# A gate table in SBUF laid out by token instead of by expert column, in a two-layer transformer kernel on one core

## Chip, cores and metric

The kernel runs on one core of a Trainium2 chip. The metric is the device time of one execution in microseconds; lower is better. Times are medians over several executions.

## The reference, cut to what matters

256 tokens of width 1024 go through two transformer blocks. The first ends with a mixture over 16,384 tiny experts (128 x 128), of which each token takes 16 for each of 8 heads:

```
experts = e1 * 128 + e2                      # 16 per token and head
g   = softmax(best)                          # their gate weights
act = gelu(x . u[experts])                   # one number for each
out = sum over experts of (g * act) * v[experts]
```

The kernel does not gather. It computes gelu(x . u) for all 128 x 128 experts, multiplies by a dense table G of gates that is zero where an expert was not chosen, and multiplies the whole by v. The second block (attention over the sequence, a gated linear attention, cross attention, a gated feed-forward) is not touched by the change.

## The kernel before

Everything is float32, and each matmul is made from three passes of rounded parts. Weights come in 404 blocks of 128 x 1024 float32 (a block is 512 KB) through a ring of four buffers. For each block ScalarE makes the rounded part (`w_hi`, L588) as soon as TensorE has freed the buffer, and the remainder (`w_lo`) is a subtraction on GpSimd (L487) for the blocks of even number in the stages below, and on VectorE (L1043) for the odd ones. In the first of the three stages below, all remainders are GpSimd's.

Experts are ordered so that partition p and column e of the table are one expert. `big` is one buffer of 128 partitions x 32,768 floats that holds G as 128 columns x 256 tokens. Three stages matter.

*The gate stage.* It builds G. For each token VectorE writes two 128 x 128 one-hot matrices (L1365, L1366); TensorE multiplies them (L2003) into a bank of PSUM, four tokens side by side, 128 columns each; ScalarE copies the bank of 512 numbers into G (L868). There are 64 such groups of four tokens. Beside it runs one block of x . u for every two groups, 32 in all (L1643), evacuated with gelu (L843) and stored to DRAM. The order on each engine is written out by hand.

*The V stage.* It takes the 64 columns whose activations are ready. Per column c: VectorE multiplies the activations of 256 tokens with column c of G (L1384), rounds the product into `h_op` (L1391) and writes the remainder (L1393); TensorE multiplies block v[c] with it in 24 matmuls (L2020). `h_op` has two buffers, so the rounding of column c waits until TensorE has finished column c - 2. ScalarE's `w_hi` waits for the same event. VectorE then does the `w_lo` of an odd block, after every second column, while GpSimd does that of the even block.

*The U and V stage.* It takes the other 64 columns: TensorE alternates between the x . u of a column (24 matmuls, L1643) and the V product of the column before (24, L2020). Gelu (L889) stands between L1643 and L1384.

Of the kernel before, what the change touches and what calls it, by code (L numbers as in the profile page):

```python
# [30 lines left out]
ACT = mybir.ActivationFunctionType  # L31
# [5 lines left out]
NQ = 256  # L37
# [14 lines left out]
PH, NKEYS, TOPK = 8, 128, 16  # L52
# [83 lines left out]
def build(nc, dram):  # L136
    ctx = ExitStack()
    with ctx:
        def sb(name, shape, dt=F32):
            return ctx.enter_context(nc.sbuf_tensor(name, shape, dt))  # L140
# [3 lines left out]
        def sem(name):  # L144
            if name not in sems:
                sems[name] = ctx.enter_context(nc.semaphore(name))
            return sems[name]
# [16 lines left out]
        big = sb("big", [P, NKEYS * NQ])  # L164

        ps = ctx.enter_context(nc.psum_tensor("ps", [P, 8, 512], F32))
# [129 lines left out]
        hf = work[:, 1].rearrange("p a b c -> p a (b c)")[:, :, 0:NQ]  # L296
        a_in = work[:, :].rearrange("p w a b c -> p (w a) (b c)")[:, :, NQ:2 * NQ]
        one1, one2 = work[:, 0], work[:, 1]
        G = big[:, :].rearrange("p (e t) -> p e t", t=NQ)

        def pcol(name, k=0, rows=P):
            return par[0:rows, PARAMS[name][0] + k:PARAMS[name][0] + k + 1]
# [278 lines left out]
        def _(act):  # L581
            def hi(n):
                s = n.mod(RING)
                act.wait_ge(sem(f"raw_loaded{s}"), n.div(RING) * 16 + 16)
                if n.first >= RING:

                    act.wait_ge(sem("block_used"), n.plus(1 - RING).value())
                act.activation(w_hi[:, s, :], raw[:, s, :], ACT.Copy).then_inc(sem("hi_done"), 1)  # L588
# [248 lines left out]
            def early(c, m):  # L837

                act.wait_ge(sem("block_used"), m.plus(B_QUERY - M_QUERY + 1).value())
                if c.first >= RING:  # L840

                    act.wait_ge(sem(f"early_stored{c.mod(RING)}"), c.div(RING) * 16)
                act.activation(a_out[:, c.mod(RING), :], ps[:, m.mod(2), 0:NQ], ACT.Gelu).then_inc(sem("bank_free"), 1)  # L843
# [20 lines left out]
            def beside(i):  # L864
                for j in range(RING):
                    for g in range(2 * j, 2 * j + 2):
                        act.wait_ge(sem("g_product"), At(g + 1, i, 8).value())
                        act.activation(G[:, :, bass.ds(At(4 * g, i, 32).value(), 4)],  # L868
                                       ps[:, 2 + g % 2, :].rearrange("p (t e) -> p e t", t=4), ACT.Copy
                                       ).then_inc(sem("g_ready"), 1)  # L870
                    hi(At(B_BESIDE + 3 + j, i, RING))
                    early(At(EARLY - EARLY_G + j, i, RING), At(M_PEER - EARLY_G + j, i, RING))

            his(B_BESIDE + 3)
            beside(0)
            with act.Fori(1, EARLY_G // RING) as i:
                beside(i)
# [153 lines left out]
        def _(dve):  # L1031
# [349 lines left out]

            def split(c, a, chunk):
                b = c.mod(2)
                dve.tensor_tensor(hf[:, b, :], a, G[:, bass.ds(chunk.value(), 1), :].rearrange("p e t -> p (e t)"),  # L1384
                                  ALU.mult).then_inc(sem("act_used"), 1)
                dve.wait_ge(sem("act_used"), c.plus(1).value())
                if c.first >= 2:

                    n = B_V + c.first - 1 if c.first < EARLY + 2 else B_PEER + 2 * (c.first - EARLY) - 1
                    dve.wait_ge(sem("block_used"), c.value(n, c.stride if c.first < EARLY else 2 * c.stride))  # L1390
                dve.tensor_copy(h_op[:, b, 0, :], hf[:, b, :]).then_inc(sem("act_hi"), 1)  # L1391
                dve.wait_ge(sem("act_hi"), c.plus(1).value())
                dve.tensor_tensor(h_op[:, b, 1, :], hf[:, b, :], h_op[:, b, 0, :].bitcast(F32), ALU.subtract  # L1393
                                  ).then_inc(sem("acts_ready"), 1)

            def early(c):
                if c.first < RING:

                    split(c, a_out[:, c.mod(RING), :], c.plus(EARLY - RING))
                else:  # L1400
                    dve.wait_ge(sem(f"early_loaded{c.mod(RING)}"), c.div(RING) * 16)
                    split(c, a_in[:, c.mod(RING), :], c.plus(-RING))
                n = At(B_V + 2 + c.first, c.i, c.stride)
                if lo_owner(n.first) == "dve":
                    lo(n)

            def chunk(d):
                dve.wait_ge(sem("gelu_done"), d.plus(1).value())
                split(d.plus(EARLY), ge[:, d.mod(2), :], d.plus(EARLY))
# [932 lines left out]
```

## Time and profile before

| what | us |
|---|---|
| median of three runs (lowest to highest) | 1535.91 (1533.37 to 1537.11) |
| the profiled execution | 1533.37 |
| its span, first to last instruction | 1531.4 |
| TensorE busy | 1436.3 |
| VectorE busy | 1058.7 |
| ScalarE busy | 684.4 |
| GpSimd busy | 678.5 |

The table shows TensorE busy in nearly all of the span. The shares are means over stages with different limits, so the rows below go by stage. An instruction's duration in the trace runs until it has ended, the time that it is held up after its start included. The profiled execution is 2.54 us below the median.

### The profile page before, as it was taken

To read this page: it belongs to the slowest core of one execution; us is meant where nothing else is said; L and a number is where in the kernel's file an instruction comes from. 1 tells how busy PE (TensorE), PEld (TensorE's weight loads), DVE (VectorE), ACT (ScalarE), POOL (GpSimd) and SP (SyncE) were. 2 spreads that over 40 slices of the span, in tenths; PEclk is the share of its full clock that TensorE was granted. 3 is DMA by queue.
4 is the path that set the end of the run, shared out by engine and by line. 5 is a ranking of instruction groups with operands and counts; after the bars stand their busy time and mean duration, and the time that the engine had idled before them with its cause. 6 is when DMAs were issued, how large, how long until landed. Compare 5 with 4: busy or idle time off the path is not lost.

```text
span 1531.4 us, 31404 instructions
## 1 busy us (share of the span) xinstructions
PE 1436.3 (94%) x11038; PEld 1351.3 (88%) x11038; DVE 1058.7 (69%) x2036; ACT 684.4 (45%) x1035; POOL 678.5 (44%) x300
## 2 busy tenths in 40 slices
PE   7999998998688889999999999999999988999997
PEld 5776588998688889999999999999999967799997
DVE  4424636889899997776665665655655755489997
ACT  4433644444244444333344444444445456555553
POOL 2313247779544434444444444444433425255442
PEclk9999989999799999999999999999999999999999
DMA  7411035666433334777755555565564324255552
GB/s 274 138 55 42 28 124 186 194 191 185 120 117 112 110 120 155 229 230 232 235 183 177 190 183 180 185 188 182 180 198 138 138 69 132 64 191 187 185 176 81
DMA packets 79624, 240.69 MB, mean 157 GB/s; under 512 B 8896, under 2 KB 25552, under 8 KB 78928
## 3 DMA queue, kind: packets, MB, share of 16 engines
q1 hardware_dynamic: 75744, 228.75, 47.3%
q10 hardware_dynamic: 3824, 11.17, 2.0%
q8 instruction: 38, 0.62, 0.2%
q14 instruction: 18, 0.15, 0.0%
HBM read 229.37 MB, written 10.52 MB: 157 GB/s over the span
## 4 chain that ended last, share of the span: by engine, by line
PE 77%; DVE 18%; issue 2%; ACT 1%; DVEq 1%; DMA 0%; POOL 0%; ACTq 0%
PE ps L1643 37%; PE ps L2020 27%; DVE work L1365 6%; DVE work L1366 2%; PE ps L1907 2%; PE ps L1861 1%; PE ps L1658 1%; DVE big L1352 1%; PE ps L1832 1%; DVE big L1350 1%; PE ps L1881 1%; DVE big L1065 1%; DVEq L1366 1%; DVE big L1354 1%; PE ps L2003 1%
## 5 line engine op out<-in xcount | busy, mean ns | idle before, releaser
L487 POOL TENSOR_TENSOR w_lo<-raw,w_hi 128x1024 fp32r<-128x1024 f32 x241 | 626.0, 2600 | 727.9 <-ACT w_hi L588 727.8
L1643 PE MATMUL ps<-x_op,w_hi 128*128 128x256 f32 (+1 forms) x3968 | 746.6, 289 | 20.8 <-DVE x_op L1061 8.8
L1643 PEld LDWEIGHTS ps<-x_op,w_hi 128*128 128x128 f32 x3968 | 627.6, 194 | 34.0 <-issue 20.9
L1643 PE MATMUL ps<-x_op,w_lo 128*128 128x256 f32 (+1 forms) x1984 | 567.5, 286 | 0.0
L588 ACT ACTIVATE w_hi<-raw 128x1024 fp32r<-128x1024 f32 x400 | 420.5, 1055 | 253.0 <-PE ps L2020 201.3
L2020 PE MATMUL ps<-h_op,w_hi 128*128 128x256 f32 x2400 | 428.5, 279 | 2.5 <-DVE h_op L1593 2.5
L1643 PEld LDWEIGHTS ps<-x_op,w_lo 128*128 128x128 f32 x1984 | 385.5, 194 | 0.0
L2020 PEld LDWEIGHTS ps<-h_op,w_hi 128*128 128x128 f32 x2400 | 368.0, 188 | 3.1 <-issue 1.9
L2020 PE MATMUL ps<-h_op,w_lo 128*128 128x256 f32 x1200 | 337.3, 281 | 0.0
L1043 DVE TENSOR_TENSOR w_lo<-raw,w_hi 128x1024 fp32r<-128x1024 f32 x159 | 206.5, 1299 | 103.0 <-ACT w_hi L588 102.9
L2020 PEld LDWEIGHTS ps<-h_op,w_lo 128*128 128x128 f32 x1200 | 225.2, 188 | 0.0
L1365 DVE TENSOR_SCALAR work<-kept,route_t 128x128 f32<-128x128 f32 x256 | 132.3, 517 | 4.6 <-PE ps L2003 2.6
L1393 DVE TENSOR_TENSOR h_op<-work,h_op 128x256 fp32r<-128x256 f32 x128 | 121.9, 952 | 4.4
L1384 DVE TENSOR_TENSOR work<-work,big 128x256 f32<-128x256 f32 x124 | 54.7, 441 | 73.6 <-ACT work L889 72.4
L2003 PE MATMUL ps<-work 128*128 128x128 f32 x512 | 71.2, 283 | 29.3 <-DVE work L1366 29.3
L1391 DVE CAST h_op<-work 128x256 fp32r<-128x256 f32 x128 | 58.5, 457 | 54.0 <-PE ps L2020 45.0
L1366 DVE TENSOR_SCALAR work<-kept,route_t 128x128 f32<-128x128 f32 x256 | 94.9, 371 | 0.0
L2003 PEld LDWEIGHTS ps<-work 128*128 128x128 f32 x512 | 62.9, 193 | 35.2 <-DVE work L1366 35.2
L889 ACT ACTIVATE work<-ps 128x256 f32<-128x256 f32 x64 | 24.7, 386 | 125.1 <-PE ps L1643 125.1
L843 ACT ACTIVATE kv_mem<-ps 128x256 f32<-128x256 f32 x64 | 24.6, 384 | 96.2 <-PE ps L1643 96.2
L868 ACT ACTIVATE big<-ps 128x512 f32 (+1 forms) x64 | 38.2, 598 | 65.3 <-PE ps L2003 65.3
L524 POOL TENSOR_TENSOR big<-big 128x544 f32<-128x544 f32 (+1 forms) x24 | 25.6, 1066 | 81.5 <-DVE big L1230 81.5
(267 smaller groups left out, 1079.8 us busy)
## 6 DMA issues: line engine op xcount, KB each, us to landing
raw<-blocks SPq DMA_DIRECT2D x404, 512.0 KB, 3.5
early_store<-kv_mem SPq DMA_DIRECT2D x60, 128.0 KB, 3.3
work<-early_store SPq DMA_DIRECT2D x60, 128.0 KB, 3.8
big<-consts ACTq DMA_DIRECT2D x2, 1336.0 KB, 6.5
big<-h_t ACTq DMA_DIRECT2D x4, 272.0 KB, 3.7
big<-bias_lines ACTq DMA_DIRECT2D x8, 136.0 KB, 2.8
bias_lines<-route_t ACTq DMA_DIRECT2D x4, 264.0 KB, 3.1
res<-mem_t SPq DMA_DIRECT2D x1, 1024.0 KB, 8.4
```

Of the source, the lines that this page charges most:

```text
L487: pool.tensor_tensor(w_lo[:, s, :], raw[:, s, :], w_hi[:, s, :].bitcast(F32), ALU.subtract).then_inc(sem("lo_pool"), 1)
L588: act.activation(w_hi[:, s, :], raw[:, s, :], ACT.Copy).then_inc(sem("hi_done"), 1)
L868: act.activation(G[:, :, bass.ds(At(4 * g, i, 32).value(), 4)], ps[:, 2 + g % 2, :].rearrange("p (t e) -> p e t", t=4), ACT.Copy).then_inc ...
L1043: dve.tensor_tensor(w_lo[:, s, :], raw[:, s, :], w_hi[:, s, :].bitcast(F32), ALU.subtract).then_inc(sem("lo_dve"), 1)
L1365: dve.tensor_scalar(one1[:, g, j, :], con("iota"), route_t[:, 0, tok], None, ALU.is_equal)
L1366: return dve.tensor_scalar(one2[:, g, j, :], con("iota"), route_t[:, 1, tok], route_t[:, 2, tok], ALU.is_equal, ALU.mult)
L1384: dve.tensor_tensor(hf[:, b, :], a, G[:, bass.ds(chunk.value(), 1), :].rearrange("p e t -> p (e t)"), ALU.mult).then_inc(sem("act_used"), 1)
L1391: dve.tensor_copy(h_op[:, b, 0, :], hf[:, b, :]).then_inc(sem("act_hi"), 1)
L1393: dve.tensor_tensor(h_op[:, b, 1, :], hf[:, b, :], h_op[:, b, 0, :].bitcast(F32), ALU.subtract).then_inc(sem("acts_ready"), 1)
L1643: mm = pe.matmul(ps[:, m_bank, 0:T], w, x, start=(k == 0 and j == 0), stop=(k == last and j == 2))
L2003: mm = pe.matmul(ps[:, 2 + g % 2, P * k:P * k + P], one1[:, g % 2, k, :], one2[:, g % 2, k, :], start=True, stop=True)
L2020: mm = pe.matmul(out, w, x, start=(first and j == 0 and k % 2 == 0), stop=(last and j == 2), skip_group_check=True)
```

## The change

G is read as 256 tokens x 128 columns instead of 128 columns x 256 tokens. ScalarE's copy then reads 512 adjacent floats of PSUM and writes 512 adjacent floats of `big`; before, it read PSUM with a step of 128 floats and wrote runs of four floats, 256 floats apart. VectorE's product (L1384) then reads its column of G with a step of 128 floats (512 bytes), where it read 256 adjacent floats. The instructions are as many as before and have as many elements.

```
-        G = big[:, :].rearrange("p (e t) -> p e t", t=NQ)
+        G = big[:, :].rearrange("p (t e) -> p t e", e=NKEYS)
...
-                        act.activation(G[:, :, bass.ds(At(4 * g, i, 32).value(), 4)],
-                                       ps[:, 2 + g % 2, :].rearrange("p (t e) -> p e t", t=4), ACT.Copy
-                                       ).then_inc(sem("g_ready"), 1)
+                        act.activation(big[:, bass.ds(At(512 * g, i, 4096).value(), 512)], ps[:, 2 + g % 2, :],
+                                       ACT.Copy).then_inc(sem("g_ready"), 1)
...
-                dve.tensor_tensor(hf[:, b, :], a, G[:, bass.ds(chunk.value(), 1), :].rearrange("p e t -> p (e t)"),
+                dve.tensor_tensor(hf[:, b, :], a, G[:, :, bass.ds(chunk.value(), 1)].rearrange("p t e -> p (t e)"),
                                   ALU.mult).then_inc(sem("act_used"), 1)
```

## Rows read from the trace of the kernel before

**Rows 1.** The page's chain that ended last, by line.
```profile
PE ps L1643 37%; PE ps L2020 27%; DVE work L1365 6%; DVE work L1366 2%; PE ps L1907 2%; PE ps L1861 1%; PE ps L1658 1%; DVE big L1352 1%; PE ps L1832 1%; DVE big L1350 1%; PE ps L1881 1%; DVE big L1065 1%; DVEq L1366 1%; DVE big L1354 1%; PE ps L2003 1%
```

**Rows 2.** Busy time by stretch: the gate, V, and U-and-V stages.
```profile
400.00:592.70 192.70, 163.41 (x1306) 157.47 (x1306) 187.73 (x516) 81.98 (x130) 79.34 (x32) 0.98 0.34 108
592.70:773.60 180.90, 180.90 (x1538) 180.90 (x1538) 125.25 (x222) 68.35 (x65) 79.66 (x32) 1.00 0.73 226
773.60:1133.30 359.70, 359.70 (x3026) 359.61 (x3026) 217.19 (x251) 149.67 (x188) 158.46 (x63) 1.00 0.59 184
```
Columns of Rows 2: us, then busy us (instructions) of PE, PEld, DVE, ACT, POOL, then PEclk, DMA share, GB/s.

**Rows 3.** Timeline of VectorE, GpSimd and ScalarE in the V stage.
```profile
706.63 0.42 DVE L1384 TENSOR_TENSOR work<-work,big 128x256 f32<-128x256 f32 x1
...
706.92 2.41 POOL L487 TENSOR_TENSOR w_lo<-raw,w_hi 128x1024 fp32r<-128x1024 f32 x1 [3.17 <-ACT w_hi L588]
...
708.61 0.87 DVE L1391 CAST h_op<-work 128x256 fp32r<-128x256 f32 x1 [1.56 <-PE ps L2020]
...
709.52 0.43 DVE L1393 TENSOR_TENSOR h_op<-work,h_op 128x256 fp32r<-128x256 f32 x1
...
709.86 1.22 DVE L1043 TENSOR_TENSOR w_lo<-raw,w_hi 128x1024 fp32r<-128x1024 f32 x1
...
711.00 0.42 DVE L1384 TENSOR_TENSOR work<-work,big 128x256 f32<-128x256 f32 x1
...
711.44 1.06 ACT L588 ACTIVATE w_hi<-raw 128x1024 fp32r<-128x1024 f32 x1 [1.77 <-PE ps L2020]
...
711.54 0.30 DVE L1391 CAST h_op<-work 128x256 fp32r<-128x256 f32 x1
...
711.87 0.43 DVE L1393 TENSOR_TENSOR h_op<-work,h_op 128x256 fp32r<-128x256 f32 x1
...
712.38 0.42 DVE L1384 TENSOR_TENSOR work<-work,big 128x256 f32<-128x256 f32 x1
...
712.58 2.49 POOL L487 TENSOR_TENSOR w_lo<-raw,w_hi 128x1024 fp32r<-128x1024 f32 x1 [3.25 <-ACT w_hi L588]
...
717.94 0.42 DVE L1384 TENSOR_TENSOR work<-work,big 128x256 f32<-128x256 f32 x1
```

**Rows 4.** Timeline in the gate stage (start us, us, engine, line).
```profile
504.35 0.35 DVE L1366 TENSOR_SCALAR work<-kept,route_t 128x128 f32<-128x128 f32 x1
...
504.49 2.50 POOL L487 TENSOR_TENSOR w_lo<-raw,w_hi 128x1024 fp32r<-128x1024 f32 x1 [3.30 <-ACT w_hi L588]
...
504.61 2.47 DVE L1365 TENSOR_SCALAR work<-kept,route_t 128x128 f32<-128x128 f32 x1
...
508.68 0.60 ACT L868 ACTIVATE big<-ps 128x512 f32 x1 [1.45 <-PE ps L2003]
```

**Rows 5.** Timeline and chain in the U-and-V stage.
```profile
855.18 2.41 POOL L487 TENSOR_TENSOR w_lo<-raw,w_hi 128x1024 fp32r<-128x1024 f32 x1 [3.11 <-ACT w_hi L588]
...
855.20 2.68 DVE L1393 TENSOR_TENSOR h_op<-work,h_op 128x256 fp32r<-128x256 f32 x1
...
859.36 2.71 PE ps L2020 x23
```

**Rows 6.** ScalarE's 512-element copies from PSUM by line: ns min/median/max.
```profile
L868 ACT ACTIVATE big<-ps x64: 591/597/602, 404.8 to 589.9; 128x512 f32 x56, 128x512 f32<-128x512 f32 x8
...
L788 ACT ACTIVATE big<-ps x24: 570/584/598, 137.5 to 1314.7; 128x512 f32<-128x512 f32 x24
```

**Rows 7.** Two-operand instructions of VectorE and GpSimd by line, ns min/median/max.
```profile
L1384 DVE TENSOR_TENSOR work<-work,big x124: 416/425/2624, 599.4 to 1133.7; 128x256 f32<-128x256 f32 x124
...
L1043 DVE TENSOR_TENSOR w_lo<-raw,w_hi x159: 1148/1218/5445, 23.4 to 1510.1; 128x1024 fp32r<-128x1024 f32 x159
...
L487 POOL TENSOR_TENSOR w_lo<-raw,w_hi x241: 2344/2487/4437, 12.8 to 1506.5; 128x1024 fp32r<-128x1024 f32 x121
```

**Rows 8.** The first product (timeline) and the last one (chain).
```profile
590.57 0.43 DVE L1384 TENSOR_TENSOR work<-kv_mem,big 128x256 f32<-128x256 f32 x1 [1.97 <-ACT big L868]
...
1133.73 0.44 DVE work L1384
```

## The prediction

> **What bounds the kernel now.** I read the page's chain first, then the busy time cut by stage, then the instructions that the change edits, and last the timelines of the stages where they run.
>
> The chain [rows 1] is TensorE's: L1643 and L2020 are 64% of the span, and VectorE's one-hots (L1365, L1366) are 8%. Neither L868 nor L1384 is in its long entries. The stretches [rows 2] say why. In the gate stage VectorE is busy 187.7 of 192.7 us and TensorE 163.4: VectorE sets that stage. In the V stage TensorE is busy for all of 180.9 us, 2.83 us for each of 64 columns, or 5.65 us for two. VectorE shows only 125.3 busy there. In the U-and-V stage TensorE is busy for all of 359.7 us.
>
> So by shares VectorE has 55 us to spare in the V stage. The timeline says otherwise [rows 3], and this is what the reader should see. Follow VectorE from the product at 706.63 to the one at 712.38. The product ends at 707.05. GpSimd's `w_lo` has begun at 706.92, and the rounding that VectorE starts at 708.61 takes 0.87 us instead of the 0.30 that the one at 711.54 takes: it ends at 709.48, just behind GpSimd's end at 709.33. While GpSimd runs, VectorE does not get through. The same is plain in the gate stage, where a one-hot that starts at 504.61, behind GpSimd's start at 504.49, takes 2.47 us and ends with it [rows 4], and in the U-and-V stage at 855.20 [rows 5]. From 709.48 on VectorE goes without a pause: remainder, `w_lo`, product, rounding, remainder (to 712.30), and the next product at 712.38. Next comes GpSimd again, at 712.58, and its end (715.07) is 2.27 us behind the end of that product (712.80), as before it was 2.28 behind (709.33 and 707.05). The VectorE loop is thus tied to itself: from 706.63 over 712.38 to 717.94 it takes 11.31 us for four columns, and TensorE needs 4 x 2.83 = 11.31. The V stage has two bounds of equal length; the time that VectorE's busy figure leaves out is GpSimd's.
>
> **The change part by part.**
>
> *ScalarE's copy, 64 times (L868).* It is 597 ns with a step of 128 floats on the PSUM side; a copy of as many elements with adjacent floats, L788, is 584 [rows 6]. So each gets 13 ns shorter, 0.8 us of ScalarE in all, and the range of L788 (570 to 598) allows from 27 shorter to 1 longer. In the gate stage two of them stand in the way from one-hots to the block's `w_hi` and so to GpSimd's start. A start 13 ns earlier than 504.49 still falls inside the one-hot that runs from 504.35 to 504.70, and GpSimd's end (506.99) is 2.29 behind that one's end, as in the V stage: VectorE loses as much as before. Cost: nothing, hidden under VectorE's one-hots. Without that cover it would be 32 x 2 x 0.013 = 0.8 us of gain.
>
> *VectorE's product, 128 times (L1384), reads with a step.* No instruction of VectorE in this trace reads that many single floats from SBUF with a step, so I bound it. From below: the copy of rows 6 reads single floats 512 bytes apart and pays 13 ns for 512, which is 7 ns for 256. A gain has no reason: the operand was adjacent. From above: a product of 256 takes 425 ns and the same form on 1024 takes 1218 [rows 7], so an element costs 793 / 768 = 1.03 ns and 256 cost 264; if every stepped element takes two turns, the product gets 264 ns longer. The lower row is another engine's on another memory, the upper one VectorE's own on the same memory, so I take a value nearer to it: two thirds, 176 ns, a product of about 600.
>
> The Trainium skill prices this case itself. "Vector Engine (DVE) Microarchitecture Reference", section 5.2, gives 1.73 ns per column when one of two sources hops at every element and 1.054 when none does. No row here shows it; by it the product would grow by 0.173 us and the sum below would be 10.0 instead of 10.2.
>
> *What 176 ns do in the V stage.* Two products lie in each pair of columns, so VectorE's loop becomes 0.352 us longer per pair, and it had nothing to spare: 32 x 0.352 = 11.3 us. The first lateness is absorbed: a column's remainder ends at 709.95, and TensorE is through with the column before only just ahead of 711.44, when ScalarE's `w_hi` follows it [rows 3]; that is 1.4 us of lead. Left: 11.3 - 1.4 = 9.9. What is late next: the following product no longer starts ahead of GpSimd (712.38 against 712.58) but behind, waits until GpSimd's end, and with it its column; lateness piles up until TensorE stalls, and with TensorE ScalarE's and GpSimd's start move too. Behind the product on VectorE are queued its own rounding and remainder and the odd `w_lo`. That `w_lo` frees the ring buffer for SyncE's next load, but it is needed some three columns later, so the loads stay hidden.
>
> *In the U-and-V stage* the remainder blocked at 855.20 ends at 857.88, and TensorE wants it at 859.36 [rows 5]: 1.48 us of lead per column, not shared with the next one, since gelu sets each product's start. 0.176 us fit. Cost: nothing; without that lead it would be 64 x 0.176 = 11.3.
>
> *The ends.* The first product waits for the last copy into G and the last for the last gelu [rows 8]; both lie on the path: 2 x 0.176 = 0.35.
>
> **Sum:** 9.9 + 0.35 = 10.2 us. The profiled execution's own time of 1533.4 becomes 1543.6. It lies 2.5 below the median of 1535.9, so as a median I forecast 1546.1.
>
> **Rivals.**
>
> *The stepped read is free, or nearly.* For it speaks ScalarE's row: 13 ns for 512 such floats. Against it, that PSUM is not SBUF. The time is then 1533.4 to 1533.9, as a median 1536. It decides below about 90 ns: 64 x 0.09 - 1.4 + 0.2 = 4.6 us, 0.3% of the time, which is about what a measurement of this kernel can tell from no change. The Trainium skill also has a sentence on this side: "VectorE: DVE Perf Modes", in the part on the plain mode, says that float32 and odd strides all work in it because it assumes nothing; read as a promise of speed, it would give this rival's 1536. No run so far shows which of the two pages holds for G.
>
> *The stall costs more than the added length.* If every stretch of GpSimd's falls where neither the wait for TensorE nor an instruction's start overlaps it, VectorE loses also what is hidden today. The rounding at 708.61 was through 0.15 us behind GpSimd, where a free one takes 0.30, so 0.15 is hidden per pair; with about as much for a wait of VectorE for TensorE that falls elsewhere it is 0.27 a pair, 32 x 0.27 = 8.6 us more: 1555 as a median, and with the upper price of 264 ns (64 x 0.264 - 1.4 + 0.5 = 16.0) 1560. For it speaks that VectorE can run at most two columns ahead; against it, that today's loop meets TensorE's to 0.01 us without any idle of TensorE.
>
> *Faster: ScalarE's copy is what the gate stage waits for.* Were its streaming part halved by adjacent access (0.2 us of 0.6) and the stage set by one-hots, product, copy, `w_hi` and GpSimd in a ring, it would win 32 x 0.2 = 6.4 us or more: 1529.5. It decides when the copy falls by more than 0.14 us, from 504.49 to before 504.35, since only then another one-hot is hit. Rows 6 allow 0.027, and VectorE has no gap between one-hots. Small.
>
> **How the numbers follow.** The forecast (product 90 to 264 ns longer, loop as summed, 1540 to 1552) gets 0.54; the costlier stall, up to 1560 and a little beyond, 0.16; the free read 0.26; the faster gate stage 0.04. Slower by over 0.3% is 0.70, within 0.3% 0.26, faster 0.04. The range reaches from 1534.5, which takes in most of the free read, to 1560, the sum of the upper bounds. The likeliest case alone is 1540 to 1552.
>
> **What would show it.** The group of L1384 should have a median near 600 ns, L868 near 584 and no change of the gate stage's length. TensorE should show idle in the V stage, put down to VectorE's `h_op`, the stage should last about 191 us, and the U-and-V stage should stay at 359.7 within 1 us. L1384 should show some instructions of over 2 us inside the V stage, where it had none. I am wrong if L1384 stays near 425 (no change), or if it is near 600 and the V stage still takes 181 (then the loop has slack that I do not see, as in the 0.17 us between remainder and product ahead of 712.38, 16 x 0.17 = 2.7 us of it at most), or if the U-and-V stage grows.

## The result, and the profile after

| | before | after |
|---|---|---|
| median us (executions) | 1535.14 (4) | 1557.05 (4) |
| ratio, with its 95% interval | | 1.0143 [1.0116, 1.0170] |
| span of the profiled execution, us | 1531.4 | 1548.2 |
| median product, ns | 425 | 639 |
| ScalarE's copy into G, ns | 597 | 597 |

The change makes the kernel 1.4% slower, some 22 us. I had forecast 10.2 and a range to 1560. The measured 1557.05 lies in the range, but the loss is more than twice the forecast.

First, the changed instructions, by line (ns min/median/max). In the changed kernel the product is L1383, its rounding L1390, its remainder L1392; L2019 is the V product and L1642 the x . u.

```profile
L868 ACT ACTIVATE big<-ps x64: 592/597/602, 404.5 to 589.7; 128x512 f32 x56, 128x512 f32<-128x512 f32 x8
```
```profile
L1383 DVE TENSOR_TENSOR work<-work,big x124: 594/639/2868, 602.2 to 1150.2; 128x256 f32<-128x256 f32 x124
```

The copy is as long as it was to the nanosecond [rows 6]; adjacent access gave it nothing. The product is 214 ns longer by the median [rows 7]; I had taken 176.

Then the same three stages by busy time, to be read against [rows 2]:

```profile
400.00:592.20 192.20, 162.89 (x1303) 156.97 (x1302) 187.50 (x516) 81.66 (x129) 79.40 (x32) 0.98 0.32 108
592.20:788.50 196.30, 183.02 (x1541) 181.02 (x1540) 168.96 (x222) 68.33 (x65) 80.39 (x32) 1.00 0.65 209
788.50:1149.80 361.30, 359.92 (x3028) 359.74 (x3026) 289.94 (x251) 149.78 (x189) 153.60 (x63) 1.00 0.59 183
```

TensorE does the same work in the V stage, but needs 196.3 us for it instead of 180.9, with 13.3 us of idle (the other 2.1 us stand as longer busy time, in a record whose matmul ends are modelled). The granted clock is 1.00 in both, so it is not the clock that lengthened this stage. The waits of this stretch name what it idled for (engine and line, what it waited for, us in total, times, longest):

```profile
DVE h_op L1390 <- PE ps L2019: 14.6, 12, 1.5
PEld ps L2019 <- DVE h_op L1392: 13.6, 9, 1.6
PE ps L2019 <- DVE h_op L1392: 13.3, 10, 1.5
```

Before, VectorE waited 45.0 us for TensorE here (31 times, 1.45 us each), and TensorE never for VectorE. All 45.0 us of these waits lay inside GpSimd's `w_lo`, by the starts and ends in the trace, which is why they were no reserve.

The timeline of VectorE and GpSimd shows what happens to the loop of [rows 3]:

```profile
643.19 0.62 DVE L1383 TENSOR_TENSOR work<-work,big 128x256 f32<-128x256 f32 x1
...
643.46 2.63 POOL L487 TENSOR_TENSOR w_lo<-raw,w_hi 128x1024 fp32r<-128x1024 f32 x1 [4.91 <-ACT w_hi L588]
...
645.12 1.12 DVE L1390 CAST h_op<-work 128x256 fp32r<-128x256 f32 x1 [1.31 <-PE ps L2019]
...
649.05 2.46 POOL L487 TENSOR_TENSOR w_lo<-raw,w_hi 128x1024 fp32r<-128x1024 f32 x1 [2.97 <-ACT w_hi L588]
...
649.33 2.67 DVE L1383 TENSOR_TENSOR work<-work,big 128x256 f32<-128x256 f32 x1
...
654.66 2.39 POOL L487 TENSOR_TENSOR w_lo<-raw,w_hi 128x1024 fp32r<-128x1024 f32 x1 [3.15 <-ACT w_hi L588]
654.68 2.51 DVE L1390 CAST h_op<-work 128x256 fp32r<-128x256 f32 x1
...
657.57 0.60 DVE L1383 TENSOR_TENSOR work<-work,big 128x256 f32<-128x256 f32 x1
...
661.67 0.63 DVE L1383 TENSOR_TENSOR work<-work,big 128x256 f32<-128x256 f32 x1
```

At 643.19 the product still starts ahead of GpSimd, as before. One pair of columns later it is too late (649.33 against 649.05) and waits until GpSimd ends. Another pair later it is the rounding (654.68) that is caught. Over the whole stage 10 products, 6 roundings and 4 remainders take over 1.9 us; before, none did. Now TensorE has run out of columns and stalls (1.43 us of idle ahead of its matmul at 657.71, put down to VectorE's L1392), with it ScalarE's `w_hi` and GpSimd's next start, and the round begins again at 661.67: 18.48 us for three pairs of columns, where TensorE needs 3 x 5.65 = 16.96.

### The profile page after: what moved, and what is told of

It reads as the page before. It is cut to its first block, busy times and chain, and to the rows that moved or that the text cites. A ratio compares the mean times of both kernels' runs of the same rounds, so it can differ in the third digit from the quotient of the medians.

```text
span 1548.2 us, 31404 instructions
## 1 busy us (share of the span) xinstructions
PE 1435.7 (93%) x11038; PEld 1350.0 (87%) x11038; DVE 1175.8 (76%) x2036; ACT 684.5 (44%) x1035; POOL 674.5 (44%) x300
## 4 chain that ended last, share of the span: by engine, by line
PE 68%; DVE 25%; issue 3%; ACT 1%; DVEq 1%; DMA 0%; POOL 0%; ACTq 0%
PE ps L1642 36%; PE ps L2019 20%; DVE work L1364 6%; DVE work L1383 3%; DVE work L1365 2%; DVE h_op L1390 2%; DVE w_lo L1042 2%; PE ps L1906 2%; PE ps L1860 1%; DVE h_op L1392 1%; PE ps L1657 1%; DVE big L1351 1%; PE ps L1831 1%; DVE big L1349 1%; PE ps L1880 1%
## 5 line engine op out<-in xcount | busy, mean ns | idle before, releaser
L1642 PE MATMUL ps<-x_op,w_hi 128*128 128x256 f32 (+1 forms) x3968 | 746.7, 289 | 21.1 <-DVE x_op L1060 8.8
L1642 PEld LDWEIGHTS ps<-x_op,w_hi 128*128 128x128 f32 x3968 | 627.8, 194 | 34.3 <-issue 21.2
L1642 PE MATMUL ps<-x_op,w_lo 128*128 128x256 f32 (+1 forms) x1984 | 567.5, 286 | 0.0
L2019 PE MATMUL ps<-h_op,w_hi 128*128 128x256 f32 x2400 | 429.3, 280 | 17.1 <-DVE h_op L1392 14.7
L1642 PEld LDWEIGHTS ps<-x_op,w_lo 128*128 128x128 f32 x1984 | 385.7, 194 | 0.0
L2019 PEld LDWEIGHTS ps<-h_op,w_hi 128*128 128x128 f32 x2400 | 367.0, 188 | 19.8 <-DVE h_op L1392 13.6
L2019 PE MATMUL ps<-h_op,w_lo 128*128 128x256 f32 x1200 | 336.2, 280 | 0.0
L2019 PEld LDWEIGHTS ps<-h_op,w_lo 128*128 128x128 f32 x1200 | 225.3, 188 | 0.0
L1392 DVE TENSOR_TENSOR h_op<-work,h_op 128x256 fp32r<-128x256 f32 x128 | 194.3, 1518 | 4.4
L1383 DVE TENSOR_TENSOR work<-work,big 128x256 f32<-128x256 f32 x124 | 99.8, 805 | 66.0 <-ACT work L888 65.0
L1365 DVE TENSOR_SCALAR work<-kept,route_t 128x128 f32<-128x128 f32 x256 | 95.4, 373 | 0.0
L1390 DVE CAST h_op<-work 128x256 fp32r<-128x256 f32 x128 | 59.4, 464 | 25.7 <-PE ps L2019 14.6
```

What stands on the lines that cost most here:

```text
L1365: return dve.tensor_scalar(one2[:, g, j, :], con("iota"), route_t[:, 1, tok], route_t[:, 2, tok], ALU.is_equal, ALU.mult)
L1383: dve.tensor_tensor(hf[:, b, :], a, G[:, :, bass.ds(chunk.value(), 1)].rearrange("p t e -> p (t e)"), ALU.mult).then_inc(sem("act_used"), 1)
L1642: mm = pe.matmul(ps[:, m_bank, 0:T], w, x, start=(k == 0 and j == 0), stop=(k == last and j == 2))
L2019: mm = pe.matmul(out, w, x, start=(first and j == 0 and k % 2 == 0), stop=(last and j == 2), skip_group_check=True)
```

## The experiments

Stage lengths below are read from first and last starts in each trace: the gate stage from the first one-hot (L1365 before) to the first V product of TensorE (L2020), the V stage from there to the next x . u of TensorE (L1643), the U-and-V stage from there to the last product of VectorE (L1384).

| kernel | gate | V | U and V | ratio, 95% interval |
|---|---|---|---|---|
| before | 192.1 | 181.0 | 360.3 | |
| after | 192.2 | 196.2 | 361.8 | 1.0143 [1.0116, 1.0170] |
| stepped read only | 192.3 | 197.6 | 361.8 | 1.0133 [1.0087, 1.0179] |
| adjacent copy only | 192.0 | 181.1 | 360.3 | 1.0004 [0.9989, 1.0019] |
| step in V stage only | 192.0 | 196.3 | 360.3 | 1.0112 [1.0085, 1.0138] |
| step in U-and-V stage only | 192.2 | 181.0 | 361.8 | 1.0008 [0.9990, 1.0027] |
| after, V stage's `w_lo` on VectorE | 190.7 | 181.1 | 361.7 | 1.0015 [1.0001, 1.0029] |
| before, V stage's `w_lo` on VectorE | 190.8 | 181.1 | 360.3 | 1.0008 [0.9995, 1.0021] |
| token pairs | 191.4 | 181.0 | 360.3 | 1.0000 [0.9979, 1.0020] |
| before with filler | 190.5 | 187.2 | 360.7 | 1.0058 [1.0040, 1.0077] |
| gate stage's `w_lo` on VectorE | 156.5 | 182.3 | 360.3 | 0.9805 [0.9789, 0.9822] |
| gate and V stage's on VectorE | 156.7 | 181.0 | 360.3 | 0.9759 [0.9718, 0.9799] |
| the same, stepped products | 156.7 | 181.1 | 361.7 | 0.9771 [0.9734, 0.9808] |

**The two halves of the change apart.**

```
+        G_step = big[:, :].rearrange("p (t e) -> p t e", e=NKEYS)
...
-                dve.tensor_tensor(hf[:, b, :], a, G[:, bass.ds(chunk.value(), 1), :].rearrange("p e t -> p (e t)"),
+                dve.tensor_tensor(hf[:, b, :], a, G_step[:, :, bass.ds(chunk.value(), 1)].rearrange("p t e -> p (t e)"),
```

> Only VectorE's product reads with the step of 128 floats; ScalarE writes G as before the change, so the products take other elements of G than the reference wants. Theory (the stepped read alone makes the product 0.21 us longer, and the V stage's loop of VectorE and GpSimd cannot absorb it): the whole loss is here, 1.011 to 1.017 of before, product median 0.64 us, copy 0.597 us, V stage 195 us. Rival (the copy's new form takes part of the loss, in the gate stage): clearly less than the change's 1.4%, under 1.008.

The other half leaves the product alone and takes the copy's two new lines from the change:

> Only ScalarE's copy is the changed one, adjacent on both sides; VectorE reads 256 adjacent floats as before, so the products take other elements of G than the reference wants. Theory: nothing, within 0.3% of before, copy 0.597 us, V stage 181 us. Rival (the copy costs or gains in the gate stage): over 0.3% in either direction, with a gate stage of another length than 188.7 us.

The whole loss is in the stepped read (1.0133), and the copy is worth nothing (1.0004). The V stage took 197.6 us, 2.6 more than I had expected. Both theories of the copy, mine of a nothing hidden under VectorE and the rival's, needed it to get shorter at all, and it did not.

**The stepped read in one stage at a time.** The view of G is chosen by the column's number:

```
+                column = G_step[:, :, bass.ds(chunk.value(), 1)] if c.first < EARLY else G[:, bass.ds(chunk.value(), 1), :]
+                column = column.rearrange("p a b -> p (a b)")
```

and with `>=` for the other kernel.

> The stepped read only in the 64 products of the V stage; the G layout written is that of before, so these products take other elements. Theory: nearly the whole loss, 1.010 to 1.016; V stage 194 to 196 us, U-and-V stage 360 to 361. Rival (the U-and-V stage has a part in it that the one profile does not show): half of the loss, about 1.007.

> The stepped read only in the 64 products of the U-and-V stage; the G layout written is that of before, so these products take other elements. Theory: within 0.3% of before; V stage 181 us, U-and-V stage 360 us, although its products take 0.64 us too. Rival: about 1.007.

The V stage has nearly all of it: 196.3 us, 1.0112. In the U-and-V stage 64 products of 0.64 us add 1.5 us in all, not 64 x 0.21 = 13.4, and this once, at its first column; I had expected nothing here. The chain of this kernel there (start us, us, what):

```profile
779.14 2.89 PE ps L1646 x24
782.03 0.02 issue
782.06 0.39 ACT work L890
...
782.47 0.65 DVE work L1387
...
783.48 2.66 DVE h_op L1396
786.14 0.14 issue
786.27 3.05 PE ps L2023 x24
```

No column is ready in advance when the stage begins, so gelu, product and remainder are on the path once, and the longer product lets GpSimd's `w_lo` in before the remainder, which is then held up: it takes 2.66 us. The timelines of GpSimd and VectorE at this door, first in this kernel, then in the kernel before, where the remainder is 0.20 us ahead:

```profile
783.47 2.38 POOL L488 TENSOR_TENSOR w_lo<-raw,w_hi 128x1024 fp32r<-128x1024 f32 x1 [6.39 <-ACT w_hi L589]
```
```profile
777.71 0.43 DVE L1393 TENSOR_TENSOR h_op<-work,h_op 128x256 fp32r<-128x256 f32 x1
...
777.91 2.49 POOL L487 TENSOR_TENSOR w_lo<-raw,w_hi 128x1024 fp32r<-128x1024 f32 x1 [6.39 <-ACT w_hi L588]
```

**GpSimd taken out of the V stage.** The owner of a remainder is one function; the rest of the edit gives the loops the same bounds.

```
 def lo_owner(n):
...
+    if B_V < n <= B_PEER + 1:
+        return "dve"
     return "pool" if B_QUERY <= n <= B_V or n % 2 == 0 else "dve"
```

> The changed kernel, with every remainder (w_lo) of the V stage on VectorE, so that GpSimd is silent there. Theory (the loss needs GpSimd's turn in VectorE's loop): VectorE's loop is then product 0.76, rounding 0.33, remainder 0.34 and w_lo 1.14 us = 2.57 per column (start to start) against TensorE's 2.83: the V stage is back at 181 to 182 us although the product still takes 0.64, the whole is within 0.3% of before (up to 1.003). Rival (VectorE was short of time by its own work alone, and gets more of it here): the V stage is longer than 196 us, the whole slower than 1.014.

> The kernel before, with every remainder of the V stage on VectorE. Theory: TensorE alone bounds the V stage then as it did before (181 us), so within 0.3% of before. Rival (the two equal bounds cost something already in the kernel before): faster by up to 2 us.

This is the sharpest of the tests. VectorE gets 32 more remainders of 1.22 us to do, the products stay at 634 ns by the kernel's median (618 in this stage), and the V stage is back at 181.1:

```profile
596.00:777.10 181.10, 181.10 (x1540) 181.10 (x1539) 158.20 (x254) 68.32 (x65) 0.00 (x0) 1.00 0.69 228
```
```profile
649.46 0.61 DVE L1387 TENSOR_TENSOR work<-work,big 128x256 f32<-128x256 f32 x1
...
650.52 0.42 DVE L1396 TENSOR_TENSOR h_op<-work,h_op 128x256 fp32r<-128x256 f32 x1
651.15 1.23 DVE L1046 TENSOR_TENSOR w_lo<-raw,w_hi 128x1024 fp32r<-128x1024 f32 x1 [0.20 <-ACT w_hi L592]
652.29 0.62 DVE L1387 TENSOR_TENSOR work<-work,big 128x256 f32<-128x256 f32 x1
```

From product to product it takes 2.83 us, TensorE's pace, with 0.2 us of waiting for ScalarE inside. What the stepped read had run into was GpSimd's turn, not VectorE's own work. In the timeline of the kernel before, 122 entries of VectorE start inside one of GpSimd's `w_lo` between 400 and 1150 us, and 120 of them end with it or after it. Of the two others, one reads an operand from PSUM (1138.62, 1.28 us), and one starts in an entry of GpSimd that takes 4.75 us, about twice the usual (405.04, 2.44 us). What the two engines share was not tested. On the kernel before the same edit changes nothing (1.0008), as it must if TensorE bounds the stage either way.

**Runs of two floats.** The layout between the two: G by pairs of tokens.

```
+        G = big[:, :].rearrange("p (q e s) -> p q e s", e=NKEYS, s=2)
...
+                        act.activation(big[:, bass.ds(At(512 * g, i, 4096).value(), 512)].rearrange("p (q e s) -> p q e s", q=2, s=2),
+                                       ps[:, 2 + g % 2, :].rearrange("p (q s e) -> p q e s", q=2, s=2),
...
+                                  G[:, :, bass.ds(chunk.value(), 1), :].rearrange("p q e s -> p q (e s)"),
```

> G laid out by pairs of tokens: pair, column, token of the pair. VectorE's product reads runs of two adjacent floats, 1024 bytes apart; ScalarE's copy reads PSUM with a step of 128 floats inside a pair and writes 512 adjacent floats. Theory A (it is single floats that cost, as the Trainium skill's Vector Engine (DVE) Microarchitecture Reference, section 5.2, has it for runs of at least two words): product 0.43 us, V stage 181, the whole within 0.3% of before. Theory B (every leap of 512 bytes or more costs): half as many leaps, product near 0.53, V stage about 187, about 1.005.

Theory A: the product is at 425 ns again, although every second float is 1024 bytes from the one before.

```profile
L1384 DVE TENSOR_TENSOR work<-work,big x124: 417/425/2626, 603.2 to 1137.5; 128x256 f32<-128x256 f32 x124
```

**Another way to lengthen VectorE's loop.**

```
+                if c.first < EARLY:
+                    for k in range(4):
+                        dve.memset(filler[:, k:k + 1], 0.0)
```

> The kernel before, adjacent reads throughout; ahead of each of the 64 products of the V stage VectorE sets four single floats (one per partition) of a buffer that nobody reads, about 0.06 us each, 0.24 us a column. Theory (the V stage's loop had no time to spare, whatever makes it longer): V stage 194 to 198 us in place of 181.0, the whole about 1.010. Rival (the stepped read itself disturbs GpSimd or TensorE at the SBUF, and VectorE's own time is not what counts): V stage within 2 us of 181.

Half a miss: the V stage is 187.2, neither 194 to 198 nor 181. My dose was wrong, and that the trace shows: the four fillers overlap each other and the product.

```profile
641.57 1.22 DVE L1044 TENSOR_TENSOR w_lo<-raw,w_hi 128x1024 fp32r<-128x1024 f32 x1
642.73 0.06 DVE L1387 MEMSET filler<- 128x1 f32 x1
642.74 0.42 DVE L1388 TENSOR_TENSOR work<-work,big 128x256 f32<-128x256 f32 x1
...
643.61 0.42 DVE L1397 TENSOR_TENSOR h_op<-work,h_op 128x256 fp32r<-128x256 f32 x1
643.98 0.06 DVE L1387 MEMSET filler<- 128x1 f32 x1
643.98 2.60 DVE L1388 TENSOR_TENSOR work<-work,big 128x256 f32<-128x256 f32 x1
```

From `w_lo` to product it is 1.17 us instead of 1.14 [rows 3], from remainder to product 0.37 instead of 0.34; where VectorE's program loop turns (661.36 to 661.97 in this trace) 0.61 instead of 0.51. That is 0.20 us for four columns, 3.2 us for the stage, and the stage got 6.2 longer, of which 5.4 are idle time of TensorE put down to VectorE. So reads by step are not needed for the loss: 0.05 us a column is enough, and it comes back about doubled.

**The step by itself.** A kernel that computes nothing of the reference times the product on idle engines.

```
+                ins = dve.tensor_tensor(result[:, 256 * (k % 8):256 * (k % 8) + 256], other[:, 0:256], table[:, 0:32768:128], ALU.mult)
```

> A kernel of its own that computes nothing of the reference: VectorE multiplies 256 adjacent floats with 256 floats of SBUF at steps of 1 to 128 floats, eight times each, GpSimd and ScalarE silent; then runs of two adjacent floats 256 apart, then copies; then ScalarE copies. Theory (the price belongs to single floats apart): about 0.42 us at a step of 1, 0.64 at 128 as in the kernel, and 0.42 for runs of two. By the Trainium skill (Vector Engine (DVE) Microarchitecture Reference, section 5.2) small steps such as 24 should cost more than far leaps (2.50 ns per column against 1.73), runs of two on an even float nothing, and on an odd one 1.30. Rival (the price in the kernel was contention): 0.42 us at every step here.

The rows are for steps of 1, 2, 3, 4, 24 and 128 floats, and for runs of two adjacent floats, 256 apart, from an even and from an odd float:

```profile
L35 DVE TENSOR_TENSOR result<-other,table x8: 416/418/425, 42.1 to 44.5; 128x256 f32<-128x256 f32 x8
...
L39 DVE TENSOR_TENSOR result<-other,table x8: 417/419/426, 44.9 to 47.3; 128x256 f32<-128x256 f32 x8
...
L43 DVE TENSOR_TENSOR result<-other,table x8: 487/494/500, 47.7 to 50.6; 128x256 f32<-128x256 f32 x8
...
L47 DVE TENSOR_TENSOR result<-other,table x8: 602/609/618, 51.1 to 54.7; 128x256 f32<-128x256 f32 x8
...
L59 DVE TENSOR_TENSOR result<-other,table x8: 794/795/798, 63.9 to 68.8; 128x256 f32<-128x256 f32 x8
...
L79 DVE TENSOR_TENSOR result<-other,table x8: 583/592/593, 86.7 to 90.2; 128x256 f32<-128x256 f32 x8
...
L83 DVE TENSOR_TENSOR result<-other,table x8: 416/418/426, 90.8 to 93.2; 128x256 f32<-128x256 f32 x8
...
L87 DVE TENSOR_TENSOR result<-other,table x8: 415/416/424, 93.6 to 96.0; 128x256 f32<-128x256 f32 x8
```

At 128 floats the step costs 592 - 418 = 174 ns with nobody else at work, so these 174 ns are no contention. The Trainium skill ("Vector Engine (DVE) Microarchitecture Reference", section 5.2) has 1.73 ns per column where one source hops 4 KiB at every element, and 1.054 where none does; the difference gives an estimate of 173 ns for 256 columns, and the trace agrees with it at this shorter hop of 512 bytes. At a step of 24 floats the page has 2.50 to 2.51, but for both sources or for the destination alone; the estimate from it is 1.45 ns a column over the adjacent read, and the trace, with one source, has (795 - 418) / 256 = 1.47. For pairs that start on an odd float the page has 1.30, again with both sources so; with one, the trace has 416 ns against 418, no cost. My expectation had left out that these two rows are not for one source.

I had expected 0.64 us at 128 floats, as in the kernel; it is 0.592. The 639 ns in the kernel are 47 more. GpSimd is not all of that: in the V stage in which it is silent the product takes 618. What adds the rest was not tried.

**The same hold-up where it costs most.** If VectorE stands still while GpSimd makes a remainder, the gate stage, where VectorE is the bound, should show it. This is no part of the change, but it tests the mechanism at 32 places at once.

```
+    if B_BESIDE <= n <= B_V:
+        return "dve"
...
                     ins.then_inc(sem("one_hot_ready"), 1)
...
+                    lo(At(B_BESIDE + 2 + q, i, RING))
```

> The kernel before, with the 32 remainders of the gate stage on VectorE in place of GpSimd. Theory (while GpSimd runs a remainder, VectorE stands still for 2.2 us of its 2.5): VectorE's round of eight tokens and one block is 8 x 0.45 + 1.14 = 4.7 us in place of 5.8, TensorE's own work 2.87 + 2 x 0.98 = 4.8, so the round takes 4.9 to 5.2 us, the gate stage 157 to 168 us in place of 188.7, the whole 0.984 to 0.988 of before. Rival (GpSimd and VectorE share, and VectorE loses nothing by it): VectorE gets 32 x 1.14 = 36 us more work and the kernel is slower by up to 2%.

The gate stage falls from 192.1 to 156.5 us and the kernel to 0.9805, both more than I had expected (157 to 168 us, 0.984 to 0.988). VectorE's eight tokens and one `w_lo` take 4.76 us from `w_lo` to `w_lo` (start us 503.08 and 507.84) instead of 5.8 (GpSimd's starts at 498.69 and 504.49 in the kernel before), and TensorE is now busy in all of the stage:

```profile
402.80:559.30 156.50, 155.85 (x1302) 154.78 (x1301) 153.04 (x548) 81.61 (x129) 4.04 (x1) 0.99 0.41 137
```
```profile
503.08 1.21 DVE L1056 TENSOR_TENSOR w_lo<-raw,w_hi 128x1024 fp32r<-128x1024 f32 x1
504.21 0.27 DVE L1380 TENSOR_SCALAR work<-kept,route_t 128x128 f32<-128x128 f32 x1
504.41 0.33 DVE L1381 TENSOR_SCALAR work<-kept,route_t 128x128 f32<-128x128 f32 x1
...
507.84 1.21 DVE L1056 TENSOR_TENSOR w_lo<-raw,w_hi 128x1024 fp32r<-128x1024 f32 x1
```

**Both stages at once, with and without the change's layout.**

> The kernel before, with the remainders of the gate stage and of the V stage all on VectorE. Theory: gate stage 156.5 us as with those of the gate stage alone, V stage 181 to 182.5, the whole 0.979 to 0.982 of before, no better than the gate stage alone, since TensorE bounds the V stage either way.

> The same on the changed kernel: stepped products of 0.64 us, GpSimd silent in the gate and V stages. Theory (the step costs only where VectorE's loop has no time to spare): within 0.3% of the kernel with the same owners and adjacent products, 0.980 to 0.984 of before. Rival (the step costs by itself): 1% slower than that.

0.9759 and 0.9771, both a little faster than I had expected: the change's layout costs no more than can be told apart once GpSimd is silent in these stages. The 1.4 us of the U-and-V stage, where GpSimd still works, remain. The first is also the best kernel of this study, but its interval overlaps with that of the gate stage alone; of the 6.8 us between the two profiled spans the V stage's 182.3 against 181.0 explains 1.3, and most of the rest lies outside the three stages. Why is open.

## Why the prediction fell short

*The bound.* Right, and it carried the forecast: VectorE's loop around GpSimd was as long as TensorE's, in spite of 55 us of idle by the busy shares. A kernel with GpSimd silent in the V stage, the step in one stage at a time, and the filler each show it.

*ScalarE's copy.* Right that it costs nothing, wrong on the 13 ns that I gave it: 597 before and after. The 584 of L788 is another place's figure, not the price of the step.

*The product.* The term was taken at 176 ns and measured 214 by the median over both stages, in the V stage from product to rounding 0.75 us where it was 0.54. The bounds from rows held (7 and 264). Of the two pages that the prediction names, the one with a price held for the step alone (174 against 173), but not for the product inside the kernel; the other, read as a promise of speed, did not hold.

*The V stage's sum.* This is the step that failed: "32 x 0.352 = 11.3" and "the first lateness is absorbed", 9.9 in all. Measured: 15.2. With 0.21 in place of 0.176 the first term is 64 x 0.21 = 13.4. The other 1.8 us are in the place of the 1.4 that I took off, a swing of 3.2. So one term was mis-sized (176 for 214 ns) and the other, the absorbed lateness, had the wrong sign. I had written the costlier stall down as a rival, and the stage behaves in part like it (its V stage would be 9.9 + 8.6 = 18.5 us longer, between which and the forecast the 15.2 lie). That the rival's 1555 comes near the measured 1557 is in part luck, since the 1557 hold 1.5 us of the U-and-V stage, and some 5 us by which the medians differ more than the profiled spans, that the rival did not have. The mechanism: VectorE is not late by a steady amount, it is caught at three different instructions, and about once in three pairs both it waits for TensorE (12 times, 14.6 us) and TensorE for it (10 times, 13.3 us). Only its own waits are hidden behind GpSimd (14.5 of the 14.6 us). The filler shows the same on its own: 3.2 us added, 6.2 lost.

*The U-and-V stage.* "Cost: nothing" was right for 63 columns and wrong for the first, which had no lead: 1.5 us. Growth of this stage was one of the signs of being wrong that I had named. The lead of 1.48 us that I read in the middle of the stage did not hold at its door.

*The ends.* 0.2 us each, as said: the last product takes 0.64 us in the changed kernel's chain where it took 0.44, and the first one 0.63 where it took 0.43 [rows 8].

The profile's span rose by 16.8 us; 15.2, 1.5 and the ends come to 17.1, so nothing else got longer in it. The medians differ by 22. The profiled execution of the changed kernel (span 1548.2 us) is shorter than that of each of the nine other executions on record (1551.0 to 1560.9). Of the remaining 5 us this is what the traces show: the kernel with the stepped read alone is 1.5 us behind the changed one at the end of the U-and-V stage. In both, TensorE's granted clock falls to the lower level at 1258 us; in the 8 us before, TensorE was busy for 6.1 us in the first kernel and 5.3 in the changed one. The first kernel spends, in two stretches, 17 and 14 us at that level (1.2 GHz of 2.4, granted clock 0.5), where the changed kernel's profile spends 7 and 7; its span is 1555.4 against 1548.2. Executions of the kernel before show the same spread, from 1532.9 us at a mean granted clock of 0.975 to 1544.0 at 0.967. Whether the changed kernel spends more time at the lower level than the kernel before was not settled; no trace shows one of its longer executions.

## What to carry to other kernels

An engine's idle time is no reserve while another engine's instruction holds it up. Follow the loop from one of its instructions to the next of the same kind and subtract nothing: if that distance equals the bounding engine's, what is added to it is paid, and more. Here 13.4 us added cost 15.2, and 3.2 us cost 6.2. And whoever turns a layout to please the writer should look at the reader: with two adjacent floats in each run the product here was as fast as with 256.

## What was not expected of the hardware

- The price of a step in SBUF is not monotone: 418 ns for 256 elements at steps of 1 and 2 floats, 494 at 3, 609 at 4, 795 at 24, 592 at 128, and nothing at all for pairs 256 floats apart.
- ScalarE pays it in SBUF and not in PSUM. In the kernel that times steps, L113 reads 256 adjacent floats of SBUF and L117 the same with a step of 128; L105 and L109 are the copy into G in its new and its old form, from PSUM (busy us, mean ns of one, idle us before):

```profile
L117 ACT ACTIVATE mirror<-table 128x256 f32<-128x256 f32 x4 | 2.2, 619 | 0.0
L105 ACT ACTIVATE mirror<-bank 128x512 f32<-128x512 f32 x4 | 2.1, 602 | 0.0
L109 ACT ACTIVATE mirror<-bank 128x512 f32<-128x512 f32 x4 | 2.1, 602 | 0.0
L113 ACT ACTIVATE mirror<-table 128x256 f32<-128x256 f32 x4 | 1.3, 404 | 0.0
```

  So ScalarE's row, which I used as the lower bound because it stepped by 512 bytes, spoke of PSUM and of runs of four written floats, and said nothing on SBUF.
- VectorE's plain copy of 256 floats goes from 286 to 439 ns with a step of 128 floats (L95 and L91 of the same kernel).
